# Token lists of a mixture-of-experts layer: scattered into a DRAM table by the router and loaded by GpSimd, in place of lists built on TensorE pass by pass

## The chip, the cores and the metric

One core of one Trainium2 chip. The metric is the device time of one execution of the program in microseconds (us); lower is better.

## The reference

One decoder layer for 512 tokens of 1024 float32 numbers. First comes RMSNorm, an input projection, differential attention and a retention group, and an output projection that is added to x. Then comes the part that the change is about, a mixture of experts:

```
logits = h2 @ w_router + b_router
top_val, top_idx = top_k(logits, 4)          # 4 of 32 experts for each token
gates = softmax(top_val)
# rows of one expert lie together, in blocks of 128 slots
h   = xb @ w_in[e] + b_in[e]                 # 1024 -> 2048
glu = min(h[:, ::2], 7); lin = clip(h[:, 1::2], -7, 7)
act = glu * sigmoid(1.702 * glu) * (lin + 1)
y   = act @ w_out[e] + b_out[e]              # 1024 -> 1024
x   = x + sum over the token's 4 experts of gate * y
```

A last RMSNorm gives the output. There are 512 x 4 = 2048 pairs of token and expert.

## The kernel before

**Stages.** The first 340 us compute attention, retention, the output projection and the router, tile by tile (4 tiles of 128 tokens). The normed rows h2 go to a DRAM table `h2_rows`. Then come the expert passes. A pass is one expert with up to 128 slots, one token in each; with these inputs there are 33 passes (32 experts, one of which needs two). Slots that no token fills are empty. After the last pass the four parts of each token are read back from DRAM, added and normed.

**A pass.** The weights of a pass come as 12 chunks of 1 MB (128 partitions x 2 x 1024 numbers): four for the first half of the up projection, four for the down projection of the pass before, four for the second half. SyncE loads them into a ring of 6 slots, each as soon as the chunk that lay there is used up (`hi_made`, `lo_made`). ScalarE rounds a chunk to float32r (`make_hi`, L1104), VectorE makes the remainder (`make_lo`, L1536), and TensorE multiplies it in 12 matmuls of 512 columns: 8 with the rounded part (L860, L862) and 4 with the remainder (L868). Three buffers of each part let ScalarE run ahead. Every engine walks its passes in a loop of its own (`by_pass`); pass 0 is written out ahead of it, so the loop does passes 1 to 32. The order on each engine is the order of the code; semaphores tie the engines together.

**The list of a pass.** Each pass needs the token, the destination row and the gate of its 128 slots, one slot on each partition. Before the change they are made a pass ahead, in five steps:
1. `prepare_list(p + 1)` on GpSimd (L1729 to L1734) copies the expert's columns out of the router's tables.
2. `slots_one_hot` on VectorE (L1520) compares them with the slot numbers: a 128 x 512 matrix of zeros and ones.
3. `token_list` on TensorE (L827) multiplies it with the four columns of `route`: four matmuls of 4 columns, into the bank that the turned rows use too.
4. `read_list` on VectorE (L1528 to L1531) reads token, destination and gate from there.
5. `gather` on GpSimd (L1748) fetches the 128 rows of h2 by an indirect DMA into `x_rows`. An empty slot fetches row 0.

TensorE turns the rows (`x_transposes`, L835) in the second half of pass p. `keep_lists` on GpSimd (L1761 to L1765) passes the destination and the gate on, through `list_mid`, until ScalarE scales the outputs (`scale_rows`, L1130) and GpSimd scatters them to DRAM (`scatter`, L1755). Destinations of empty slots are out of bounds and are skipped there.

**Router tiles.** In the loop over tiles, VectorE picks the four experts (L1454 to L1459), computes the gates and the columns of `route` (L1461 to L1476); TensorE counts places with triangular matmuls (L778), and VectorE reads them (`read_places`, L1379). After the last tile VectorE makes the table of passes (L1481 to L1512); GpSimd reads it by register loads (`expert_of`).

**Work space.** `work` and `operands` are two views that lie over each other in on-chip memory; x_rows, y_rows and the router's tables are pieces of `work`.

## Time and profile before

| what | value |
|---|---|
| median of 3 executions | 1586.2 us (1584.41 to 1587.89) |
| the profiled execution's own time | 1586.68 us |
| its span in the trace | 1584.9 us |
| TensorE matmul busy | 1506.2 us, 95% of the span |
| VectorE, ScalarE, GpSimd busy | 1321.6, 1008.4, 377.9 us |
| mean granted TensorE clock | 0.967 of full speed |
| passes 1 to 32, time of one | 36.29 us |
| moved by DMA | 476.46 MB |

The span is the time between the first and the last record of the trace; the execution's own time is 1.8 us more. Matmuls are pipelined, so a busy row says that TensorE had work, and the distance between the starts of two matmuls says what one costs.

### The profile page before, as it was taken

To read this page: it belongs to the slowest core of one execution; us is meant where nothing else is said; L and a number is where in the kernel's file an instruction comes from. 1 tells how busy PE (TensorE), PEld (TensorE's weight loads), DVE (VectorE), ACT (ScalarE), POOL (GpSimd) and SP (SyncE) were. 2 spreads that over 40 slices of the span, in tenths; PEclk is the share of its full clock that TensorE was granted. 3 is DMA by queue.
4 is the path that set the end of the run, shared out by engine and by line. 5 is a ranking of instruction groups with operands and counts; after the bars stand their busy time and mean duration, and the time that the engine had idled before them with its cause. 6 is when DMAs were issued, how large, how long until landed. Compare 5 with 4: busy or idle time off the path is not lost.

```text
span 1584.9 us, 23779 instructions
## 1 busy us (share of the span) xinstructions
PE 1506.2 (95%) x7537; PEld 1245.8 (79%) x7537; DVE 1321.6 (83%) x1278; ACT 1008.4 (64%) x898; POOL 377.9 (24%) x382
## 2 busy tenths in 40 slices
PE   7999689979999999999999999999999999999993
PEld 6999368737888888888888888888888888888882
DVE  5641761478999999999999999999999999999998
ACT  5221541236777777777777777777777777777773
POOL 1000301001222233223223222232232232222321
PEclk9999789959999999999999999999999999999997
DMA  9300701018999999999999999999999999999996
GB/s 295 110 1 6 260 1 47 28 42 308 358 365 369 367 369 368 369 375 368 376 360 363 368 366 368 381 358 370 370 380 367 358 365 363 367 373 373 363 375 258
DMA packets 139365, 476.46 MB, mean 301 GB/s; under 512 B 10604, under 2 KB 27272, under 8 KB 139272
## 3 DMA queue, kind: packets, MB, share of 16 engines
q1 hardware_dynamic: 128096, 445.17, 74.7%
q0 software_dynamic: 10496, 28.74, 5.3%
q10 hardware_dynamic: 744, 2.17, 0.3%
q8 instruction: 18, 0.29, 0.1%
q14 instruction: 11, 0.09, 0.0%
HBM read 463.45 MB, written 21.50 MB: 306 GB/s over the span
## 4 chain that ended last, share of the span: by engine, by line
PE 90%; DVE 4%; DMA 3%; issue 2%; ACT 2%; POOL 0%; SPq 0%; DVEq 0%; POOLq 0%; ACTq 0%
PE pair L860 23%; PE pair L868 23%; PE pair L862 23%; PE pair L748 4%; PE pair L604 3%; PE pair L605 3%; PE pair L609 3%; PE pair L875 2%; PE pair L835 2%; PE pair L886 2%; PE pair L827 1%; DMA ring<-in_w_in 1%; PE pair L797 1%; DMA gain_row<-in_ret_norm_g 1%; DVE row_max L1281 1%
## 5 line engine op out<-in xcount | busy, mean ns | idle before, releaser
L1536 DVE TENSOR_TENSOR split<-ring,split 128x2048 fp32r<-128x2048 f32 x396 | 895.0, 2287 | 44.9 <-ACT split L1104 44.8
L1104 ACT CAST split<-ring 128x2048 fp32r<-128x2048 f32 x396 | 757.8, 1914 | 228.4 <-PE pair L868 221.1
L860 PE MATMUL pair<-split,operands 128*128 128x512 f32 x1584 | 633.6, 400 | 2.6 <-DVE operands L1557 1.7
L862 PE MATMUL pair<-split,operands 128*128 128x512 f32 x1584 | 621.1, 392 | 0.0
L868 PE MATMUL pair<-split,operands 128*128 128x512 f32 x1584 | 431.9, 395 | 0.0
L868 PEld LDWEIGHTS pair<-split,operands 128*128 128x128 f32 x1584 | 295.6, 188 | 72.9 <-DVE split L1536 9.2
L860 PEld LDWEIGHTS pair<-split,operands 128*128 128x128 f32 x1584 | 298.5, 188 | 63.9 <-issue 2.2
L862 PEld LDWEIGHTS pair<-split,operands 128*128 128x128 f32 x1584 | 298.5, 188 | 61.0
L1755 POOL DMA_INDIRECT expert_rows<-work,dest_cur x33 | 77.8, 2357 | 372.9 <-PE pair L868 358.3
L1748 POOL DMA_INDIRECT work<-h_rows,token_next x34 | 76.5, 2249 | 301.8 <-DVE token_next L1531 301.8
L604 PE MATMUL pair<-split,operands 128*128 128x256 f32 x352 | 86.1, 282 | 3.1 <-DVE work L1267 3.1
L605 PE MATMUL pair<-split,operands 128*128 128x256 f32 x352 | 85.9, 282 | 0.0
L1110 ACT CAST operands<-pair 128x512 fp32r<-128x512 f32 x66 | 38.7, 587 | 73.3 <-PE pair L868 40.9
L1729 POOL COPY first_cur<-work 128x1 f32 (+1 forms) x34 | 65.6, 1930 | 42.9 <-issue 34.4
L1741 POOL CAST operands<-work 64x128 fp32r x34 | 73.9, 2172 | 1.0 <-PE pair L868 1.0
L604 PEld LDWEIGHTS pair<-split,operands 128*128 128x128 f32 x352 | 67.0, 190 | 3.3 <-DVE work L1267 3.3
L1267 DVE TENSOR_SCALAR work<-pair,stat 128x256 f32<-128x256 f32 x24 | 11.6, 483 | 67.3 <-PE pair L609 67.2
L605 PEld LDWEIGHTS pair<-split,operands 128*128 128x128 f32 x352 | 67.0, 190 | 0.0
L748 PE MATMUL pair<-late_ring,work 128*128 128x256 f32 x256 | 60.5, 400 | 1.7 <-issue 0.8
L998 ACT ACTIVATE work<-pair,stat 128x256 f32<-128x256 f32 x24 | 11.4, 473 | 79.6 <-PE pair L609 75.2
L1761 POOL CAST dest_cur<-list_mid 128x1 int32<-128x1 f32 x33 | 23.3, 706 | 154.3 <-DMA expert_rows<-work,dest_cur 154.3
L748 PEld LDWEIGHTS pair<-late_ring,work 128*128 128x128 f32 x256 | 51.6, 203 | 9.9 <-issue 1.2
(229 smaller groups left out, 1340.9 us busy)
## 6 DMA issues: line engine op xcount, KB each, us to landing
ring<-in_w_moe_in SPq DMA_DIRECT2D x264, 1024.0 KB, 7.9
ring<-in_w_moe_out SPq DMA_DIRECT2D x132, 1024.0 KB, 8.8
ring<-in_w_in SPq DMA_DIRECT2D x12, 1024.0 KB, 9.6
ring<-expert_rows SPq DMA_DIRECT2D x3, 2048.0 KB, 9.1
late_ring<-in_w_o SPq DMA_DIRECT2D x4, 1024.0 KB, 9.6
resid<-in_x SPq DMA_DIRECT2D x4, 512.0 KB, 5.3
h_rows<-work ACTq DMA_DIRECT2D x4, 512.0 KB, 2.6
late_ring<-expert_rows SPq DMA_DIRECT2D x4, 512.0 KB, 5.4
```

The costliest lines, as they stand in the source:

```text
L604: pe.matmul(dst, hT_hi[:, k, at_i], w_hi[s][:, k, :], start=(k == 0), stop=False)
L605: pe.matmul(dst, hT_lo[:, k, at_i], w_hi[s][:, k, :], start=False, stop=False)
L748: mm = pe.matmul(dst, mixT[:, i % 2, k, :], slot(s)[:, k, :], start=(k == 0), stop=(k == KT - 1))
L860: pe.matmul(dst[:, f, :], left_hi[:, k0 + k, :], hi[c.buffer][:, k, cols], start=(start and k == 0), stop=False)
L862: pe.matmul(dst[:, f, :], left_lo[:, k0 + k, :], hi[c.buffer][:, k, cols], start=False, stop=False)
L868: mm = pe.matmul(dst[:, f, :], left_hi[:, k0 + k, :], lo[c.buffer][:, k, cols], start=False, stop=(stop and k == 1))
L1104: act.copy(hi[c.buffer], raw[c.slot]).then_inc(hi_made, 1)
L1536: dve.tensor_tensor(lo[c.buffer], raw[c.slot], hi[c.buffer].bitcast(F32), ALU.subtract).then_inc(lo_made, 1)
L1729: chain(pool.tensor_copy(first_cur[:, :], col(pass_first, p)))
L1741: pool.tensor_copy(pick_bias[0:2 * NE, :], col(expert_rows, e).to_broadcast([2 * NE, SLOTS]))\
L1748: pool.indirect_dma_start(out=x_rows, out_offset=None, in_=h2_dram, in_offset=bass.IndirectOffsetOnAxis(ap=token_next[:, 0:1], axis=0))\
L1755: pool.indirect_dma_start(out=y_dram, in_=y_rows, in_offset=None, out_offset=bass.IndirectOffsetOnAxis(ap=dest_cur[:, 0:1], axis=0), bound ...
```

## The change

**Router.** For each token and each of its four picks, VectorE now computes one entry's address in a DRAM table `slot_lists` (32 experts x 512 rows of 4 words: token, destination, gate, unused): `of_rank`, a 128 x 4 x 32 comparison, replaces the columns of `route`; `place_entries` multiplies it with places and gates (two operations of 128 x 128), sums over experts, and copies the sums out. GpSimd clears the table at the start and scatters the entries by 16 indirect DMAs (four a tile) of 128 entries of 16 bytes. The table of passes gets a second row, `pass_list`, the first row of the list of a pass.

**Passes.** `prepare_list`, `slots_one_hot`, `token_list`, `read_list` and `keep_lists` are gone. GpSimd loads the token column two passes ahead (`load_tokens`: 128 pieces of 4 bytes, 16 bytes apart) and destination and gate for the pass (`load_list`: 128 pieces of 8 bytes); the gather runs two passes ahead of its pass, after TensorE has turned the rows of the pass before. It has a bound now, so empty slots fetch nothing; `x_rows` is cleared once.

**Place.** `work` and `operands` begin directly behind `resid` instead of behind some small tensors.

The diff, cut to its core:

```diff
+        lists_dram = nc.dram_tensor("slot_lists", [LIST_ROWS, 4], I32, kind="Internal").ap()
...
         resid = sb("resid", [P, NT, D])
+        with nc.sbuf_tensor("operands", [P, 20480], F32R) as operands:
+            pass
+        work = sb("work", [P, 21504])
...
-            def token_list(p):
-                pe.wait_ge(onehot_ready, p + 1)
-                for i in range(NT):
-                    mm = pe.matmul(bank[6][:, 0:4], onehot[:, i, :], route_cur[:, i, :],
-                                   start=(i == 0), stop=(i == NT - 1))
-                mm.then_inc(list_ready, 1)
...
                     act_transposes(p - 1, 1)
-                token_list(p + 1)
                 up(p, 0, 3)
...
                 up(p, 1, 1)
-                pe.wait_ge(idx_ready, p + 2)
                 x_transposes(p + 1, 0)
...
-                act.wait_ge(lists_kept, p + 1)
+                act.wait_ge(list_loaded, p * 16)
...
+            def place_entries(i):
+                for a, of_expert_at in enumerate((slot_of, gates)):
+                    chain(dve.tensor_tensor(chosen[:, a], of_rank, of_expert_at[:, i, :].unsqueeze(1).to_broadcast([P, TOPK, NE]),
+                                            ALU.mult))
+                chain.settle()
+                chain(dve.tensor_reduce(chosen_sum, chosen, AX_X, ALU.add))
+                chain.settle()
+                dve.tensor_copy(entry_at[:, i, :], chosen_sum[:, 0, :]).then_inc(entries_ready, 1)
+                dve.tensor_copy(entries[:, i, :, 2].bitcast(F32), chosen_sum[:, 1, :]).then_inc(entries_ready, 1)
...
                 if i:
                     read_places(i - 1)
+                    place_entries(i - 1)
...
                 make_lo(p, 2)
-                slots_one_hot(p + 1)
                 swiglu(p - 1, 1)
                 make_lo(p, 3)
                 make_lo(p, 4)
-                read_list(p + 1)
...
+            def place_entries(i):
+                pool.wait_ge(entries_ready, 2 * (i + 1))
+                for r in range(TOPK):
+                    pool.indirect_dma_start(out=lists_dram, in_=entries[:, i, r, :], in_offset=None,
+                                            out_offset=bass.IndirectOffsetOnAxis(ap=entry_at[:, i, r:r + 1], axis=0))\
+                        .then_inc(entries_placed, 16)
...
+            def load_tokens(p, n):
+                if n is None:
+                    pool.wait_ge(gathered, 16 * p)
+                    pool.sem_inc(pool_passed, 1)
+                c = n or 0
+                pool.dma_start(token_next[:, c:c + 1], list_of(p)[:, 0:1]).then_inc(tokens_loaded, 16)
+
+            def load_list(p):
+                if not (isinstance(p, int) and p == 0):
+                    pool.wait_ge(scattered, p * 16)
+                    pool.sem_inc(pool_passed, 1)
+                pool.dma_start(list_cur[:, :], list_of(p)[:, 1:3]).then_inc(list_loaded, 16)
+
+            def gather(p, n=0):
+                pool.wait_ge(tokens_loaded, 16 * (p + 1))
                 wait(pool, x_transposed, 2 * p)
                 pool.sem_inc(pool_passed, 1)
                 pool.indirect_dma_start(out=x_rows, out_offset=None, in_=h2_dram,
-                                        in_offset=bass.IndirectOffsetOnAxis(ap=token_next[:, 0:1], axis=0))\
-                    .then_inc(gathered, 16)
+                                        in_offset=bass.IndirectOffsetOnAxis(ap=token_next[:, n:n + 1], axis=0),
+                                        bounds_check=SEQ - 1, oob_is_err=False).then_inc(gathered, 16)
...
             def one_pass(p):
                 following = expert_of(p + 1)
-                prepare_list(p + 1, following)
-                gather(p + 1)
                 scatter(p - 1)
                 pick(p + 1, following)
-                pool.wait_ge(scattered, p * 16)
-                pool.sem_inc(pool_passed, 1)
-                keep_lists(True)
+                load_list(p)
+                load_tokens(p + 2, None)
+                gather(p + 2)
```

Before pass 0 GpSimd now does: `place_entries(3)`, the wait for all 16 scatters, `load_tokens(0)`, `gather(0)`, `load_tokens(1)`, `pick(0)`, `load_list(0)`, `gather(1)`, `load_tokens(2)`, `pick(1)`, `gather(2)`.

**Order on TensorE**, first half of a pass of the loop (L860/L862 now L848/L850, L868 now L856, L886 now L874). Before:

```order
L868 MATMUL pair<-split,operands 128x512 x4
L884 ISA
L886 MATMUL pair<-cst,work 128x128 x4
L825 REGISTER_ALU
L827 MATMUL pair<-operands 128x4 x4
L860 MATMUL pair<-split,operands 128x512
```

Now:

```order
L856 MATMUL pair<-split,operands 128x512 x4
L872 ISA
L874 MATMUL pair<-cst,work 128x128 x4
L848 MATMUL pair<-split,operands 128x512
L850 MATMUL pair<-split,operands 128x512
```

The four matmuls of the token list are gone; the turned activations are followed by the next chunk.

**Order on GpSimd**, one pass of the loop (value loads, register steps and branches stand as rows of their own). Before, from the copies of `prepare_list` to `keep_lists`:

```order
L1731 COPY pos_cur<-work 128x4
L128 ISA
L1734 TENSOR_SCALAR slot_from<-pos_cur,first_cur 128x4
L1745 REGISTER_ALU
L128 REGISTER_ALU
L1748 DMA work<-h_rows,token_next 128x1024
L1755 DMA expert_rows<-work,dest_cur 2048x1024
L1739 ISA
L1741 ISA
L1741 COPY operands<-work 64x128
L1773 REGISTER_ALU
L1761 CAST dest_cur<-list_mid 128x1
```

Now, from the scatter to the load of the tokens and the gather:

```order
L1749 DMA expert_rows<-work,list_cur 2048x1024
L1719 ISA
L1721 ISA
L1721 COPY operands<-work 64x128
...
L1736 DMA list_cur<-slot_lists 128x2
...
L1714 TENSOR_LOAD pass_list
L1714 ISA x2
L1730 ISA
L1730 DMA token_next<-slot_lists 128x1
L1739 ISA
L128 REGISTER_ALU
L1742 DMA work<-h_rows,token_next 128x1024
```

The gather stood ahead of the scatter and now stands behind it, at the end of the pass, behind two small loads.

**Order on VectorE**, end of the last router tile. Before:

```order
L1467 RECIPROCAL work<-work 128x1
L1469 TENSOR_SCALAR work<-work 128x32
L1470 TENSOR_SCALAR work<-work 128x32
L1472 TENSOR_SCALAR work<-work 128x32
L1474 CAST work<-work 128x32
L1476 TENSOR_TENSOR work<-work 128x32
L1379 SCALAR_TENSOR_TENSOR work<-pair,work 128x32
L1382 TENSOR_SCALAR work<-work 128x32
L1481 COPY work<-pair 128x32
```

Now:

```order
L1467 RECIPROCAL work<-work 128x1
L1468 TENSOR_TENSOR work<-work 128x128
L1471 TENSOR_SCALAR work<-work 128x32
L1366 SCALAR_TENSOR_TENSOR work<-pair,work 128x32
L1369 TENSOR_TENSOR work<-work 128x32
L1375 TENSOR_TENSOR work<-work 128x128 x2
L1378 TENSOR_REDUCE work<-work 128x8
L1380 CAST work<-work 128x4
L1381 COPY work<-work 128x4
L1477 COPY work<-pair 128x32
```

Four operations of 32 columns give way to one of 128; five operations of `place_entries` now stand between the places and the table of passes.

## Rows read from the trace of the kernel before

**Rows 1.** Stretch, then PE, PEld, DVE, ACT, POOL busy us, clock, DMA share, GB/s.
```profile
600.00:1000.00 400.00, 400.00 (x1853) 327.59 (x1852) 374.32 (x287) 296.56 (x210) 115.43 (x110) 1.00 0.97 368
805.00:810.00 5.00, 5.00 (x23) 3.88 (x22) 5.00 (x3) 4.01 (x3) 0.00 (x0) 1.00 1.02 417
...
340.00:350.00 10.00, 8.51 (x13) 3.24 (x12) 7.39 (x15) 5.50 (x3) 2.96 (x11) 0.50 0.11 25
```

**Rows 2.** Who waited for whom, 600 to 1400: total us, times, longest us.
```profile
ACT split L1104 <- PE pair L868: 145.8, 199, 1.3
...
DVE operands L1520 <- POOL slot_from L1734: 18.5, 22, 0.8
...
PEld pair L868 <- DVE split L1536: 6.5, 22, 0.3
```

**Rows 3.** Chain that ended last, in pass 1: start us, us, what.
```profile
393.16 0.44 PE pair L886 x4
393.60 0.34 PE pair L827 x4
393.94 0.34 PE pair L860
...
411.45 0.24 PE pair L860
```

**Rows 4.** The same chain in pass 32: two lo groups.
```profile
1529.62 0.92 PE pair L868 x4
...
1532.37 1.06 PE pair L868 x4
```

**Rows 5.** GpSimd's timeline, one pass: start us, us, instruction [idle before <-releaser].
```profile
811.12 2.39 POOL L1755 DMA_INDIRECT expert_rows<-work,dest_cur  x1 [11.17 <-PE pair L868]
...
821.01 0.19 POOL L1761 CAST dest_cur<-list_mid 128x1 int32<-128x1 f32 x1 [5.18 <-DMA expert_rows<-work,dest_cur]
...
822.73 2.13 POOL L1729 COPY first_cur<-work 128x1 f32 x1 [1.05 <-issue]
...
833.95 2.28 POOL L1748 DMA_INDIRECT work<-h_rows,token_next  x1 [8.32 <-DVE token_next L1531]
847.41 2.40 POOL L1755 DMA_INDIRECT expert_rows<-work,dest_cur  x1 [11.18 <-PE pair L868]
```

**Rows 6.** DMA issues of the page, median us to landing.
```profile
h_rows<-work ACTq DMA_DIRECT2D x4, 512.0 KB, 2.6
```

**Rows 7.** The gathers' landing time, over all 34.
```profile
DMA to landing us min/median/max: 4.4/10.0/10.7
```

**Rows 8.** TensorE's timeline in the same pass as rows 5: the row turns.
```profile
849.80 0.60 PE L835 MATMUL pair<-cst,work 128*128 128x128 f32 x4
```

**Rows 9.** DMA packets by queue, 800 to 1200.
```profile
q0 software_dynamic: 3168, 8.73, 6.1%
```

**Rows 10.** VectorE's timeline ahead of the expert loop.
```profile
315.53 0.69 DVE L1430 COPY work<-pair 128x512 f32<-128x512 f32 x1 [1.10 <-PE pair L762]
...
334.93 0.23 DVE L1469 TENSOR_SCALAR work<-work 128x32 f32<-128x32 f32 x1
...
336.11 0.19 DVE L1379 SCALAR_TENSOR_TENSOR work<-pair,work 128x32 f32<-128x32 f32 x1
...
340.25 0.19 DVE L1512 TENSOR_SCALAR pass_expert<-pair 1x50 int32<-1x50 f32 x1
```

**Rows 11.** GpSimd's timeline there.
```profile
341.33 0.18 POOL L1729 COPY first_cur<-work 128x1 f32<-128x1 f32 x1 [8.51 <-DVE pass_expert L1512]
...
347.24 1.07 POOL L1748 DMA_INDIRECT work<-h_rows,token_next  x1 [4.31 <-DVE token_next L1531]
```

**Rows 12.** TensorE's timeline in pass 0.
```profile
355.38 0.80 PE L860 MATMUL pair<-split,operands 128*128 128x512 f32 x1 [0.82 <-DVE operands L1541]
...
373.46 0.66 PE L886 MATMUL pair<-cst,work 128*128 128x128 f32 x4 [0.81 <-DVE work L1552]
```

**Rows 13.** Chain that ended last, in pass 0.
```profile
367.83 9.89 DMA work<-h_rows,token_next
```

More of the change, by code:

```diff
@@ L164, in build @@
         last_pass = sb("last_pass", [1, 1], I32)
-        pos_cur = sb("pos_cur", [P, NT])
-        slot_from = sb("slot_from", [P, NT])
-        first_cur = sb("first_cur", [P, 1])
-        token_next = sb("token_next", [P, 1], I32)
-        list_next = sb("list_next", [P, 2])
-        list_mid = sb("list_mid", [P, 2])
-        dest_cur = sb("dest_cur", [P, 1], I32)
-        gate_cur = sb("gate_cur", [P, 1])
-        work_margin = sb("work_margin", [P, 8])
-        with nc.sbuf_tensor("work", [P, 21504], F32) as work:
-            pass
-        operands = sb("operands", [P, 20480], F32R)
+        pass_list = sb("pass_list", [1, IN_TABLE], I32)
+        token_next = sb("token_next", [P, 2], I32)
+        list_cur = sb("list_cur", [P, 2], I32)
+        dest_cur, gate_cur = list_cur[:, 0:1], list_cur[:, 1:2].bitcast(F32)
         def slot(n):
@@ L844, in _ @@
             bias_product(2)
-            token_list(0)
             bias_product(3)
@@ L1781, in _ @@
-            pool.wait_ge(b_in_rounded, 1)
-            pick(0, first)
-            gather(0)
-            pool.sem_inc(gather_started, 1)
-            load_pass_count(pool)
-            keep_lists(False)
-            following = expert_of(1)
-            prepare_list(1, following)
-            gather(1)
-            pool.wait_ge(lists_kept, 1)
-            keep_lists(True)
-            pick(1, following)
-            start = chain.n
-            chain.n = 0
-            def counted_pass(p):
-                chain.before = start + (p - 1) * STEPS_TO_ROUTE
-                one_pass(p)
-                assert chain.n == STEPS_TO_ROUTE, chain.n
@@ L1801, in _ @@
-            by_pass(pool, counted_pass)
-            scatter(after_last(pool) - 1)
-            pool.sem_inc(rows_sent, 1)
+                load_list(p)
+                load_tokens(p + 2, None)
+                gather(p + 2)
+            with nc.allow_non_contiguous_dma(reason="a few hundred words"):
+                place_entries(NT - 1)
+                pool.wait_ge(table_ready, 2)
+                pool.wait_ge(entries_placed, 16 * NT * TOPK)
+                load_tokens(0, 0)
+                first = expert_of(0)
+                gather(0)
+                load_tokens(1, 1)
+                pool.sem_inc(gather_started, 1)
+                pool.wait_ge(experts_listed, 2)
+                pool.wait_ge(b_in_rounded, 1)
+                pick(0, first)
+                load_pass_count(pool)
+                load_list(0)
+                gather(1, 1)
+                load_tokens(2, None)
+                following = expert_of(1)
+                pick(1, following)
+                gather(2)
+                by_pass(pool, one_pass)
+                done = after_last(pool)
+                scatter(done - 1)
+                pool.sem_inc(rows_sent, 1)
+                pool.wait_ge(gathered, 16 * (done + 2))
```

141 lines of the change are left out of this document (58 added, 83 removed).

## The prediction

> **What bounds the kernel now.** I read the busy times by stretch first. From 600 to 1000 TensorE is busy without a gap at full clock, VectorE for 374 of 400 us, and the DMA engines show a share of 0.97 at 368 GB/s [rows 1]. Three resources look full, so the busy shares can't decide. The waits inside the loop can: ScalarE waits for TensorE before 199 chunks, 145.8 us in 800, and for no DMA at all [rows 2]. A weight that came late would show there as a wait of ScalarE's cast for SyncE's queue. So weights are early, and what TensorE executes sets the length of a pass. TensorE itself waits in one place only: once a pass (22 times in 22 passes) a weight load of the remainder group waits up to 0.3 us for VectorE [rows 2]. I then read the chain that ended last, to price single steps on TensorE, and GpSimd's timeline of one pass, whose two scatters give the pass: 847.41 - 811.12 = 36.29 us [rows 5].
>
> **The change part by part.** The sum is made against the profiled execution's own 1586.7 us, which is 0.5 us over the median of 1586.2.
>
> *Token list off TensorE, passes 1 to 32.* In the chain the four matmuls take 0.34 us, and the product behind them starts with 0.34 us where behind the plain turns it starts with 0.24 [rows 3]. So a list costs 0.34 + 0.10 = 0.44 us, and 32 of them 14.1 us. As TensorE is the bound and ran without a gap, this comes off in full, as long as nothing else becomes late.
>
> *The stall on VectorE.* The remainder groups take 0.92 us in the chain, and once a pass one takes 1.06 [rows 4]. That is 0.14 us, 4.5 us over 32 passes. VectorE is behind there since it runs back to back from the list's one-hot on. The change takes the one-hot (0.6 us) and the three small reads (0.35 us) from it, and the 0.8 us in which it waits for GpSimd's copies [rows 2]: it comes to the first remainder after the activation some 1.7 us earlier, and 0.3 us is what it lacks. I take the 4.5 us as gained. Bounds: nothing, if the backlog builds up elsewhere; 0.30 x 32 = 9.6 us, if the whole wait shown is lost time.
>
> *Two small loads a pass, and the gather behind them.* GpSimd scatters at 811.12, copies the bias column, and finds the scatter landed at 821.0 [rows 5]. Then it loads the list and the tokens. A register load and the start of the next instruction take about 1.1 us, and an instruction of GpSimd in the loop some 2.1 to 2.4 us [rows 5]. So the token load is issued by about 821 + 2 x 3.3 = 827.6. The trace shows no such small load; its landing lies between the 2.6 us of a store in a quiet stretch [rows 6] and the 10.7 us of the slowest gather under load [rows 7]. Taking a gather's 10.0, as the load shares its queue and the same busy engines: 837.6, gather issued 837.8, landed 847.8. TensorE turns the rows at 849.80 [rows 8]; the new order leaves that place in the pass as it is. So even the slow end holds by 2 us, and the quick end by 9. Cost: nothing. What hides it is the pass itself; without that cover every microsecond late is one a pass. Queued behind the gather on GpSimd is the next scatter, at 847.41, by when GpSimd has issued the gather 7 us ago. The list for ScalarE is wanted a pass later.
>
> *The gather skips empty slots, and runs a pass earlier.* Of 34 x 128 = 4352 rows some 2050 to 2200 remain, about 9 MB of 476. In the loop the gather is issued at 833.95, lands 10.0 us later and is wanted at 849.80 [rows 5, 7, 8]: it was hidden by 6 us. Nothing is gained but DMA load. A pass would ask for 13.36 - 0.27 = 13.09 MB in 35.71 us, 367 GB/s, where it now moves 368 [rows 1]: the shorter pass and the skipped rows cancel.
>
> *Pass 0.* The second gather is issued at 367.83, late, since its list waits for TensorE; its 9.89 us lie on the chain [rows 13], and TensorE, through with its chunk at 376.65 (373.46 [rows 12], 0.44 for the turns [rows 3] and 2.75 for a chunk, the distance of the two groups [rows 4]), stands for 1.2 us. Now it is issued by about 357: gain 1.2 us. Ahead of that TensorE waits 0.81 us for VectorE's activation [rows 12]; VectorE gets there 0.85 us sooner without its wait for the list. Together 2.0 us.
>
> *Ahead of the passes.* The clock is at 0.50 of full speed here, the 1.2 GHz level, and the DMA share 0.11 [rows 1]. VectorE first. Its operations take 0.19 us for 32 columns and 0.69 for 512 [rows 10], so about 0.29 for 128 and 0.42 for 256; `place_entries` is then 0.2 + 0.29 + 0.42 + 0.1 + 0.17 and three hand-overs of 0.04, 1.3 us. In tiles 1 and 2 it falls into a gap of 1.1 us [rows 10] and shows with 0.2 each; in tile 3 it shows in full, less 0.24, for the dropped columns (334.93 to 336.11 [rows 10]) make room only until TensorE's places are there. With 0.25 us for `pass_list` the table of passes comes 1.7 us later than 340.44 [rows 10]. TensorE's bias products start there, and without the token list between them (0.94 us) end 0.7 us later. By this path the first product starts at 356.1 instead of 355.38 [rows 12]. Now the rows: VectorE gives the last entries free at about 337.9, GpSimd issues four scatters of 1.07 us [rows 11], 342.2, the last lands 3.3 us later (the quickest gather's 4.4 less its issue [rows 7, 11]), 345.5. A register load, 0.9 us (340.44 to 341.33 [rows 10, 11]), then the load of the tokens, 2.6 to 4.4 us [rows 6, 7], then the gather, 4.5: landed at 353.5 to 355.3, first product 2.4 us after that, 355.9 to 357.7. So the cost is 0.7 to 2.3 us; I take 1.5. If GpSimd needs its loaded 2.3 us for each scatter instead of 1.07, add 4.9. The clearing of the table and the longer start on GpSimd (some 1.6 us) lie beside TensorE's output product.
>
> The trace's quickest landings of 2.6 and 4.4 us [rows 6, 7] are the prices I used. The Trainium skill, "DMA: Bandwidth & Descriptors", section "Anatomy of one DMA — SWDGE (gpsimd) path", gives a DMA from GpSimd about 2.0 us plus bytes / 436e3; worked out from it, as an estimate, scatter and load would land in 2.0 us each, and the start would cost 0.7 us instead of 1.5.
>
> *Place of the work space, one-hot, copies.* No row shows an effect of an address on a duration, so I take 0 for the place, with nothing on either side. GpSimd's copies, VectorE's and the waits on them were hidden, but for what is counted.
>
> **The sum.** 1586.7 - 14.1 - 4.5 - 2.0 + 1.5 = 1567.6, some 1567 against the median.
>
> **The rivals.**
> *R1, the stall stays.* VectorE is limited by ScalarE's casts, which follow TensorE, and could end up as late. Then 1586.7 - 14.1 - 2.0 + 1.5 = 1572. For it: 0.14 us is little and the engines are tied; against it: the 1.7 us that it gains.
> *R2, a slow start.* Scatters at 2.3 us each, or slow landings: 5 to 6 us more, 1573, and 1577 if R1 holds too.
> *R3, DMA becomes the bound, slower.* The loads add 256 small packets a pass and 32 for the semaphores. Packets of GpSimd's queue take 6.1% of 16 x 400 us over 3168 packets, 0.123 us each [rows 9]. If a 4-byte packet takes as much as that, 288 x 0.123 / 16 = 2.2 us of all engines a pass come in, and 66 x 0.123 / 16 = 0.5 go out. With a share of 0.97 now [rows 1], 36.29 x 0.97 + 1.7 = 36.9 us would be the pass: +0.6 x 32 = 19 us, 1586.7 + 19 - 0.5 = 1605. It decides where a small packet takes over 0.06 us. Against it: a third of that queue's packets are already small and fill, the share is counted with waiting packets, and there are stretches of 417 GB/s [rows 1].
> The rows can't price a 4-byte packet. The Trainium skill, same page, section "Specifications", wants at least 512 B, below which an engine reads, modifies and writes, and its section "Rules for kernel authors" warns that a strided last dimension becomes one descriptor for each element, as both new loads have it; that speaks for R3.
> *R4, the tokens come late, slower.* If load and gather take over 22 us from 827.6 on, TensorE waits each pass. At 3 us late: 32 x (3 - 0.6) = +77, 1663. Only a landing over 12 us does it; the slowest gather of 34 took 10.7 [rows 7].
> *R5, nothing comes of it.* TensorE's time is filled by another wait (VectorE is busy for 0.94 of the loop): 1585.
>
> **How the numbers follow.** A measurement of this kernel can tell 0.2%, 3.2 us. Chances: forecast 0.58, R1 0.17, R2 0.09, R3 0.08, R4 0.04, R5 0.04. Faster: 0.58 + 0.17 + 0.09 and 0.02 of R5, 0.86; same 0.02; slower 0.12. The range runs from 1561 (the whole 0.3 us stall gained, start at its cheap end: 1586.7 - 14.1 - 9.6 - 2.0 + 0.7 = 1561.7) to 1577 (R1 and R2 together), and leaves out R3 to R5.
>
> **What would show it.** Right: scatters 35.7 us apart in GpSimd's timeline; no remainder group over 0.92 us and no wait of the weight load for VectorE; ScalarE's casts still waiting for TensorE alone; no gap of TensorE near 377; the first product of pass 0 at 356 to 358. Wrong: a wait of the casts for SyncE's queue (R3), of L835's successor for the gather in the loop (R4), four scatters of 2.3 us before pass 0 (R2), a pass of 35.85 (R1). The forecast falls if a pass stays at 36.2 or more.

## The result, and the profile after

| | before | after |
|---|---|---|
| median of the executions | 1587.05 us (1584.41 to 1589.94, 4) | 1565.45 us (1562.15 to 1567.91, 4) |
| ratio to before, 95% interval | | 0.9854, 0.9837 to 0.9870 |
| the profiled execution's own time | 1586.68 us | 1565.79 us |
| its span | 1584.9 us | 1563.9 us |
| a pass, from scatter to scatter | 36.30 us | 35.48 us |
| first product of pass 0 starts | 355.38 us | 363.81 us |
| GpSimd busy | 377.9 us | 220.3 us |
| moved by DMA | 476.46 MB | 467.61 MB |

The change is 1.5% faster. The forecast was 1567 (1561 to 1577), faster. The pass is the mean over 12 scatters from 800 on: (1232.60 - 806.83) / 12 = 35.48. So 32 x 0.82 = 26 us come off in the loop. In these two profiles the first product comes 8.4 us later, of which pass 0 returns 2.9; how much of the 8.4 is the change's is worked out below.

The windows of the changed kernel answer to rows 1 (PE, PEld, DVE, ACT, POOL, clock, DMA share, GB/s):

```profile
60.00:150.00 90.00, 90.00 (x752) 90.00 (x751) 35.77 (x43) 18.78 (x22) 0.00 (x0) 1.00 0.08 24
600.00:1000.00 400.00, 400.00 (x1849) 330.86 (x1848) 372.17 (x250) 303.48 (x215) 52.91 (x57) 1.00 1.00 370
```

The second row looks like the one of before: TensorE full, VectorE 372 of 400, DMA now at 1.00. The first row is one that the prediction never looked at. In the input projection TensorE got through 752 matmuls in 90 us, where the kernel before got through 767:

```profile
60.00:150.00 90.00, 90.00 (x767) 90.00 (x766) 34.50 (x41) 19.04 (x22) 0.00 (x0) 1.00 0.08 24
```

No line of that stage was edited. Only its operands lie elsewhere, and the granted clock was 1.00 in both stretches.

The waits in the loop of the changed kernel, 600 to 1400, in the columns of rows 2:

```profile
ACT split L1091 <- PE pair L856: 130.2, 204, 0.9
POOL work L1742 <- DMA token_next<-slot_lists: 124.8, 22, 6.0
DVE split L1518 <- ACT split L1091: 50.4, 68, 1.1
```

These are three of its lines. The casts of the weights wait for TensorE as before, and for no DMA. The waits of the weight load and of VectorE for GpSimd are gone. GpSimd's timeline of one pass, against rows 5:

```profile
806.83 1.35 POOL L1749 DMA_INDIRECT expert_rows<-work,list_cur  x1 [16.64 <-PE pair L856]
808.15 0.34 POOL L1721 CAST operands<-work 64x128 fp32r x1
816.74 0.58 POOL L1736 DMA_DIRECT2D list_cur<-slot_lists  x1 [8.26 <-issue]
818.12 0.56 POOL L1730 DMA_DIRECT2D token_next<-slot_lists  x1 [0.79 <-issue]
824.42 1.24 POOL L1742 DMA_INDIRECT work<-h_rows,token_next  x1 [5.75 <-DMA token_next<-slot_lists]
842.32 1.34 POOL L1749 DMA_INDIRECT expert_rows<-work,list_cur  x1 [16.65 <-PE pair L856]
```

The token load is issued 11.3 us after the scatter, not 16.5 as I had it, because an instruction of GpSimd takes 0.34 to 1.35 us here and not 2.1 to 2.4. The gather lands some 8 us later (median 8.1 in this stretch), 10 us before the next scatter.

Ahead of pass 0 time was lost. The chain that ended last there (start us, us, what; short links left out at the dots):

```profile
343.46 0.51 DVE work L1375 x2
343.99 0.43 DVE work L1378
...
344.70 0.27 issue
344.96 1.00 POOL slot_lists L1695
345.96 0.30 issue
...
348.80 3.62 DMA slot_lists<-work
352.51 0.51 POOLq L1714
...
353.46 0.55 issue
354.03 1.87 DMA token_next<-slot_lists
...
356.03 0.54 issue
...
356.79 4.29 DMA work<-h_rows,token_next
...
361.22 1.94 PE pair L824 x8
363.16 0.85 PE pair L863 x2
```

It is the path of the prediction: four scatters, the last landing, the register, the token load, the gather, the turns. The scatters stand 1.27 us apart and not 1.07 (0.96 for one, 0.30 between two), and 0.55 us pass ahead of the token load and of the gather each.

### The profile page after: what moved, and what is told of

Its sections match the earlier page's. It is cut to its first block, busy times and chain, and to the rows that moved or that the text cites. A ratio compares the mean times of both kernels' runs of the same rounds, so it can differ in the third digit from the quotient of the medians.

```text
span 1563.9 us, 23287 instructions
## 1 busy us (share of the span) xinstructions
PE 1483.7 (95%) x7401; PEld 1237.8 (79%) x7401; DVE 1294.1 (83%) x1151; ACT 1009.3 (65%) x898; POOL 220.3 (14%) x237
## 2 busy tenths in 40 slices
DMA packets 142278, 467.61 MB, mean 299 GB/s; under 512 B 15702, under 2 KB 32370, under 8 KB 142185
## 4 chain that ended last, share of the span: by engine, by line
PE 90%; DVE 3%; DMA 3%; ACT 2%; issue 2%; POOL 0%; SPq 0%; POOLq 0%; DVEq 0%; ACTq 0%
PE pair L848 23%; PE pair L850 23%; PE pair L856 23%; PE pair L745 4%; PE pair L601 3%; PE pair L602 3%; PE pair L606 3%; PE pair L824 2%; PE pair L863 2%; PE pair L874 2%; DMA ring<-in_w_in 1%; DMA gain_row<-in_ret_norm_g 1%; DVE row_max L1268 1%; PE pair L767 0%; PE pair L794 0%
## 5 line engine op out<-in xcount | busy, mean ns | idle before, releaser
L848 PE MATMUL pair<-split,operands 128*128 128x512 f32 x1584 | 631.0, 398 | 1.7 <-DVE operands L1539 1.7
L850 PE MATMUL pair<-split,operands 128*128 128x512 f32 x1584 | 618.9, 391 | 0.0
L856 PE MATMUL pair<-split,operands 128*128 128x512 f32 x1584 | 424.4, 390 | 0.0
L856 PEld LDWEIGHTS pair<-split,operands 128*128 128x128 f32 x1584 | 297.5, 188 | 63.2
L848 PEld LDWEIGHTS pair<-split,operands 128*128 128x128 f32 x1584 | 298.2, 188 | 61.3 <-issue 2.2
L850 PEld LDWEIGHTS pair<-split,operands 128*128 128x128 f32 x1584 | 298.4, 188 | 58.6
L1749 POOL DMA_INDIRECT expert_rows<-work,list_cur x33 | 44.7, 1353 | 513.9 <-PE pair L856 507.9
L601 PE MATMUL pair<-split,operands 128*128 128x256 f32 x352 | 88.1, 287 | 3.4 <-DVE work L1254 3.4
L602 PE MATMUL pair<-split,operands 128*128 128x256 f32 x352 | 87.8, 286 | 0.0
L1097 ACT CAST operands<-pair 128x512 fp32r<-128x512 f32 x66 | 38.8, 588 | 74.4 <-PE pair L856 41.4
L1736 POOL DMA_DIRECT2D list_cur<-slot_lists x33 | 19.1, 580 | 267.9 <-issue 267.9
L1111 ACT CAST operands<-pair 128x512 fp32r<-128x512 f32 x66 | 38.6, 584 | 24.5 <-PE pair L874 24.5
L1534 DVE SCALAR_TENSOR_TENSOR work<-work 128x512 f32<-128x512 f32 x66 | 45.7, 692 | 6.9
```

The lines of the kernel that those rows point to most:

```text
L601: pe.matmul(dst, hT_hi[:, k, at_i], w_hi[s][:, k, :], start=(k == 0), stop=False)
L602: pe.matmul(dst, hT_lo[:, k, at_i], w_hi[s][:, k, :], start=False, stop=False)
L848: pe.matmul(dst[:, f, :], left_hi[:, k0 + k, :], hi[c.buffer][:, k, cols], start=(start and k == 0), stop=False)
L850: pe.matmul(dst[:, f, :], left_lo[:, k0 + k, :], hi[c.buffer][:, k, cols], start=False, stop=False)
L856: mm = pe.matmul(dst[:, f, :], left_hi[:, k0 + k, :], lo[c.buffer][:, k, cols], start=False, stop=(stop and k == 1))
L1534: dve.scalar_tensor_tensor(result, gate, ACT_LIMIT, line, ALU.min, ALU.mult).then_inc(act_ready, 1)
```

## The experiments

Each kernel is the changed one with the edit shown, but for the first, which is the kernel before. A difference of two kernels is taken from their ratios to the kernel before, or from the pass where the loop alone is meant; a pass repeats within 0.02 us from profile to profile where nothing touched it.

### The place alone

```diff
 resid = sb("resid", [P, NT, D])
+with nc.sbuf_tensor("operands", [P, 20480], F32R) as operands:
+    pass
+work = sb("work", [P, 21504])
...
-with nc.sbuf_tensor("work", [P, 21504], F32) as work:
-    pass
-operands = sb("operands", [P, 20480], F32R)
```

> The kernel before with nothing but the new place of work and operands. Theory P (the place sets TensorE's pace): the input projection takes 283 ns a matmul instead of 279 and GpSimd's row loads of norm2 start 3.8 us later, as in the changed kernel, and a chunk of 12 matmuls takes 2.72 us instead of 2.75; scatters 36.0 us apart, total 1587 + 3.8 - 10 = about 1581. Theory L (the lighter loop makes the matmuls quicker and the early 3.8 us are scatter between programs): both stay as before, 1587.

Measured: 1592.23 us, ratio 1.0020 (1.0003 to 1.0036); 752 matmuls in the projection, as in the changed kernel. So the projection's slower pace is the place's; as the pass is unchanged, the whole loss, 0.20% or 3.2 us (0.5 to 5.7), lies ahead of the loop. The chunks of the loop went from 2.75 to 2.72 us, but the pass stayed at 36.31: the stall grew. Waits, 600 to 1400:

```profile
PEld pair L867 <- DVE split L1535: 11.0, 22, 0.5
PEld pair L885 <- DVE work L1551: 2.3, 15, 0.2
```

6.5 us before, 13.3 now. A quicker TensorE would catch up with VectorE sooner; that fits, but no run varied it by itself.

### The change at the old place

```diff
-with nc.sbuf_tensor("operands", [P, 20480], F32R) as operands:
-    pass
-work = sb("work", [P, 21504])
...
+with nc.sbuf_tensor("work", [P, 21504], F32) as work:
+    pass
+operands = sb("operands", [P, 20480], F32R)
```

> The changed kernel with work and operands back at their old address. Theory P: the projection gains its 3.8 us back (279 ns), the loop goes to 2.75 us a chunk and 35.75 us a pass: 1565.5 - 3.8 + 8.5 = about 1570. Theory L: 1565.5, a pass stays at 35.49 us.

Measured: 1568.74 us, ratio 0.9880 (0.9863 to 0.9897), 767 matmuls, chunks of 2.75 us, no wait of a weight load. The pass is 35.69 us, what the prediction's terms give (35.71), and the first product comes at 358.66. So the place gives 0.21 us a pass once the stall is gone. Against the changed kernel the ratio is 0.0026 higher, 4.1 us, where the loop alone gives 6.7; so the place takes some 2.6 us ahead of the passes, in line with the run above. The two first products lie 5.1 us apart, but that is one profile against another, with different granted clocks (see the account of the prediction).

### The four matmuls back

```diff
                 if before:
                     act_transposes(p - 1, 1)
+                    for i in range(NT):
+                        pe.matmul(bank[6][:, 0:4], xT_hi[:, i, :], xT_lo[:, i, 0:4], start=(i == 0), stop=(i == NT - 1))
                 up(p, 0, 3)
```

> The changed kernel with four matmuls of 4 columns at the place of the token list in passes 1 to 32, with nothing to wait for (their product is not used). If the list's cost was TensorE's time alone, 0.44 us a pass: 1565.5 + 14.1 = 1579.6 and scatters 35.93 us apart. If its cost was what hung on it (the waits of other engines), under 5 us more.

Measured: 1579.28 us, ratio 0.9931 (0.9916 to 0.9946), a pass of 35.90 us. The list's matmuls cost 0.42 us, 13.4 us in all, though nobody waits for them. The timeline shows it (products between them left out): from the turns to the next remainder group 2.72 us, where the changed kernel takes 2.28.

```profile
829.88 0.60 PE L874 MATMUL pair<-cst,work 128*128 128x128 f32 x4
830.24 0.59 PE L890 MATMUL pair<-operands 128*128 128x4 f32 x4
...
832.60 1.07 PE L856 MATMUL pair<-split,operands 128*128 128x512 f32 x4
```

### VectorE's work back, without its wait

```diff
                 make_lo(p, 2)
+                chain(dve.tensor_tensor(spare, pass_number.to_broadcast([P, 512]), pass_number.to_broadcast([P, 512]), ALU.is_equal))
                 swiglu(p - 1, 1)
                 make_lo(p, 3)
                 make_lo(p, 4)
+                for n in range(3):
+                    chain(dve.tensor_scalar(spare[:, n:n + 1], pass_number, 1.0, None, ALU.add))
```

> The changed kernel with one operation of 128 x 512 at the place of the one-hot and three of one column at the place of the list's reads on VectorE, without any wait on GpSimd (their results are not used). If VectorE's backlog made the stall, part of it comes back: weight loads wait for VectorE's remainder once a pass, a remainder group takes over 0.92 us, and the total is 2 to 4.5 us over 1565.5. If the 0.8 us in which it waited for GpSimd was what made it late, nothing comes back: 1565.5.

Measured: 1564.49 us, ratio 0.9846 (0.9829 to 0.9862), a pass of 35.48. VectorE is busy 380 of 400 us, and TensorE waits for it nowhere. By itself the work that the change takes off VectorE was worth nothing.

### And its wait for GpSimd

```diff
+                dve.wait_ge(copied, 4 * p)
...
+            def make_copies():
+                for n in range(4):
+                    pool.tensor_copy(copies[:, n:n + 1], pass_number).then_inc(copied, 1)
...
                 load_tokens(p + 2, None)
+                pool.wait_ge(copied, 4 * p)
+                pool.sem_inc(pool_passed, 1)
+                make_copies()
                 gather(p + 2)
```

The first line stands ahead of the 128 x 512 operation of the run above.

> The changed kernel with VectorE's one-hot and three small operations back, as in the run before, and now also four small copies on GpSimd ahead of the gather, for which the one-hot waits. Theory, the stall of the kernel before was made by VectorE's wait for GpSimd and not by its extra work (which alone cost nothing, 1564.5): the wait of 0.1 to 0.8 us once a pass returns, with it a wait of a weight load for VectorE of up to 0.3 us, and a remainder group of 1.03 to 1.06 us: +0.14 x 32 = 4.5 us, 1570. Rival, the stall needed the token list's coupling of TensorE to VectorE (bank read, list): no remainder group over 0.92, 1565.

Measured: 1576.38 us, ratio 0.9933 (0.9908 to 0.9957), a pass of 35.79, +0.31. Waits, 600 to 1400:

```profile
DVE work L1552 <- POOL copies L1762: 12.6, 23, 2.3
PEld pair L859 <- DVE split L1521: 8.7, 22, 0.8
```

Once a pass the weight load waits again, and the timeline has a group of 1.04 us (838.41 to 839.45, where others take 0.91; rows between left out):

```profile
835.60 1.07 PE L859 MATMUL pair<-split,operands 128*128 128x512 f32 x4
...
838.41 1.20 PE L859 MATMUL pair<-split,operands 128*128 128x512 f32 x4
839.45 0.62 PE L866 MATMUL pair<-operands 128*128 128x512 f32 x2
```

VectorE does the same work as in the run above. New are the wait, 0.55 us on the mean, and the four small copies on GpSimd that it waits for. So this wait, on top of that work, makes such a stall, and the rival (that the list's bank is needed for it) falls. A run with the wait and without the work was not made. The price is near twice what I expected. One long wait is not the reason: of twelve passes one takes 36.39 us, the other eleven 35.74 on the mean, 0.26 more than without the wait, while VectorE waits 0.43 to 0.46 us in nine of the ten passes from 786 to 1108. The reason is nearer the place: the 0.14 us were read at the old place, and at the new one the kernel before stalls more (the run with the place alone: 36.31 - 35.48 - 0.42 = 0.41 us a pass).

### All rows gathered

```diff
+            pool.memset(no_entries.rearrange("p (n c) -> p n c", c=4)[:, :, 0].bitcast(F32), 0.0).then_inc(tokens_named, 1)
```

> The changed kernel with the empty slots' token set to 0, so that every gather moves all 128 rows again (34 x 128 = 4352 rows in place of some 2100, +9 MB). Theory, the skip is worth nothing because the gather is hidden and weights are early: 1565.5 within 3 us, no wait of ScalarE's casts for a DMA, gathers in the loop landing at 8 to 10 us in place of 8.1. Rival, the skip is what keeps the shorter pass within the DMA engines' reach (share 1.00 at 370 GB/s in the loop): casts wait for SyncE's queue and the pass grows from 35.49 towards 35.49 x 377/370 = 36.2 us, 1587.

Measured: 1564.98 us, ratio 0.9855 (0.9829 to 0.9881), a pass of 35.48, 377 GB/s at a share of 1.00, no wait of a cast for a DMA. The skip of empty slots is worth nothing, and a share of 1.00 at 370 GB/s isn't the limit of the DMA engines.

### Four more small loads a pass

```diff
                 pool.dma_start(token_next[:, c:c + 1], list_of(p)[:, 0:1]).then_inc(tokens_loaded, 16)
+                if n is None:
+                    for m in range(4):
+                        pool.dma_start(more[:, m:m + 1], lists_dram[0:SLOTS, m % 3:m % 3 + 1]).then_inc(more_loaded, 16)
```

> The changed kernel with four more loads of 128 x 4 bytes a pass on GpSimd's queue (512 more small packets beside 256). It prices a small packet. Theory, small packets fit between the large ones and weights have room: 1565.5 within 3 us, pass 35.49 us, no DMA wait; the token load and the gather land later by a few us, still hidden. Rival, by the price of my prediction, 0.123 us a packet on 16 engines: 512 x 0.123 / 16 = 3.9 us of all engines a pass; with the share at 1.00 now, all of it would be lost, 32 x 3.9 = +126 us, 1691; half that price still gives 1628.

Measured: 1560.72 us, ratio 0.9827 (0.9802 to 0.9852), its interval overlaps that of the changed kernel; a pass of 35.48 again. The packets of GpSimd's queue, 800 to 1200, first the changed kernel, then this one:

```profile
q0 software_dynamic: 3872, 5.80, 4.1%
```

```profile
q0 software_dynamic: 5424, 5.99, 4.4%
```

These 400 us cut passes differently in the two profiles (5.80 and 5.99 MB). Over twelve whole passes of each, 806.83 to 1232.60 and 800.43 to 1226.20, the queue has 4224 and 5760 packets at 4.1% and 4.3%: 48 loads bring 1536 packets, 32 for a load and not 128, though it has 128 pieces of 4 bytes. They take 0.2% of 16 x 426 us, some 0.009 us a packet (0.004 to 0.013, as the shares are rounded), a tenth or less of the price that the rival used and about a seventh of the 0.06 at which it decides. The small pieces that the Trainium skill warns of ("DMA: Bandwidth & Descriptors", "Rules for kernel authors") are harmless at this number: by the rows, five such loads a pass cost no time.

### 64 and 128 bytes further

```diff
 resid = sb("resid", [P, NT, D])
+place_margin = sb("place_margin", [P, 16])
 with nc.sbuf_tensor("operands", [P, 20480], F32R) as operands:
```

> The changed kernel with work and operands 64 bytes further (131264 in place of 131200); the old place was 142400. It tells what in the place sets TensorE's pace. Theory A, the position within 128 bytes: the old place and this one are both 64 past a multiple of 128, so the input projection goes back to 279 ns a matmul and 767 matmuls in 60 to 150, the loop to chunks of 2.75 us, total near that of the run at the old place, 1568.7. Theory B, something coarser (the distance from the split parts, or the region): 283 ns, 752 matmuls and 2.72 us stay, 1565.5.

> The changed kernel with work and operands 128 bytes further (131328), the one remainder of 256 not yet seen (0). Seen so far, address by remainder: 64 gives 767 matmuls and 2.75 us a chunk, 128 gives 752 and 2.72, 192 gives 797 and 2.80. If projection and chunk always trade places, 0 gives either more than 797 with over 2.80 (slower, over 1586) or under 752 with under 2.72; if the pattern is one of 128 bytes with a coarser part on top, about 752 to 760 and 2.72 to 2.74, 1565 to 1572. No theory here says which; the run fills the table.

Measured: 1585.91 us, ratio 0.9979 (0.9963 to 0.9996), and 1585.89, ratio 0.9987 (0.9975 to 1.0000). An empty margin of 64 bytes eats nearly the whole change. Windows of the 64-byte run:

```profile
60.00:150.00 90.00, 90.00 (x797) 90.00 (x796) 36.09 (x44) 19.07 (x22) 0.00 (x0) 1.00 0.08 24
600.00:1000.00 400.00, 400.00 (x1809) 323.59 (x1808) 366.40 (x243) 296.32 (x210) 54.21 (x55) 1.00 0.99 362
```

And two remainder groups of neighbouring chunks in its loop, 2.80 us apart, where the changed kernel's are 2.72 apart:

```profile
827.78 1.09 PE L857 MATMUL pair<-split,operands 128*128 128x512 f32 x4
...
830.58 1.09 PE L857 MATMUL pair<-split,operands 128*128 128x512 f32 x4
```

The projection is quicker than anywhere (797), the pass slower (36.30 us; 36.19 in the 128-byte run, whose projection has 761). The output projection doesn't take part: its matmuls take 395 ns in place of 409, but the run with all rows gathered and the one with four more loads, both at the changed kernel's place, have 395 too. In them the granted clock from 270 to 320 was 1.00, where the changed kernel's profile has 0.86. Position within 128 bytes (theory A of the first text) is refuted: the old place shares it with the 64-byte run and has neither its 797 nor its 2.80 us. So is a coarse cause.

### The projection's weights alone moved

Here and below, the weights of a matmul are the 128 x 128 operand that a weight load puts into TensorE. In the input projection these are the turned input rows (hT), in the expert passes the turned rows and activations (xT, actT); the numbers of the layer's own weight matrices stream past them.

```diff
-hT_hi, hT_lo = (operands[:, a:a + KT * SEQ].rearrange("p (k t) -> p k t", k=KT) for a in (12288, 16384))
+hT_hi, hT_lo = (operands[:, a:a + KT * SEQ].rearrange("p (k t) -> p k t", k=KT) for a in (12240, 16336))
```

> The changed kernel with only the turned rows of the input projection (hT_hi, hT_lo, the matmuls' weights there) 192 bytes earlier, so that they lie 192 past a multiple of 256 bytes as in the run with the 64-byte shift; the expert passes' operands stay. Theory, the pace of a stage follows where its own matmul weights begin, in steps of 64 bytes: the projection goes to 797 matmuls in 60 to 150 (752 now), later stages start 5 to 6.5 us earlier (norm2's load at about 258.5 in place of 264.63), chunks stay at 2.72 us: 1565.5 - 6 = 1559.5. Rival, something else in the moved region sets it (results, tables, other tensors): 752 matmuls, 1565.

Measured: 1558.06 us, ratio 0.9793 (0.9779 to 0.9807), below the interval of the changed kernel. The projection has 796 matmuls in its 90 us, the pass stays at 35.48, GpSimd's load of the gains of the second RMSNorm (L1661), the first mark behind attention, starts at 259.14 in place of 264.63, the first product at 359.04 in place of 363.81.

```profile
60.00:150.00 90.00, 90.00 (x796) 90.00 (x795) 36.39 (x45) 19.48 (x23) 0.00 (x0) 1.00 0.08 24
```

### The expert operands moved back inside the 64-byte shift

```diff
 def halves(a):
-    return operands[:, a:a + KT * SLOTS].rearrange("p (k t) -> p k t", k=KT)
+    return operands[:, 48 + a:48 + a + KT * SLOTS].rearrange("p (k t) -> p k t", k=KT)
...
-b_in_parts = operands[:, 4096:4096 + 2 * FF]
+b_in_parts = operands[:, 4144:4144 + 2 * FF]
...
-pick_bias = operands[:, 6144:6144 + SLOTS]
+pick_bias = operands[:, 6192:6192 + SLOTS]
```

> The run with the 64-byte shift once more, but the expert passes' own operands (the turned rows and activations, xT and actT, and the bias parts and pick) another 192 bytes further inside it, so that they start 256 bytes behind where the changed kernel has them, while everything else keeps the 64-byte shift. It tells whose place sets the chunk's pace. Theory, the place of the matmul's weights: chunks back at 2.72 us, the pass 35.5 us, the projection still at 797 matmuls in 60 to 150; the 64-byte shift then keeps its earlier start alone: 1585.9 - 32 x 0.82 = 1560, at best 1556. Rival, another tensor in the moved region (bank results' readers, the activations' rows, the tables behind): chunks stay at 2.80 us, the pass at 36.3 us, 1586.

Measured: 1554.57 us, ratio 0.9810 (0.9768 to 0.9852), a pass of 35.47, chunks of 2.72, the projection still at 797. Together with the run before: of the moved region, the place of the matmuls' own weights sets the pace, stage by stage. The bias parts and the pick moved with them here, but no matmul of a chunk reads those. All that was seen, by where the stage's weights start (remainder of the address by 256 bytes):

| remainder | matmuls of the projection, 60 to 150 | a chunk of the loop, us |
|---|---|---|
| 0 (128-byte run) | 761 | 2.80 |
| 64 (old place) | 767 | 2.75 |
| 128 (changed kernel) | 752 | 2.72 |
| 192 (64-byte run) | 797 | 2.80 |
| the projection's alone at 192 | 796 | 2.72 |
| the operands' alone at 128 | 797 | 2.72 |

The remainder is a label and not a mechanism: what is best for the projection (192) is worst for the loop. Why is open; which bytes other engines touch at that time was not varied. Remainder 64 was seen only at the old place, 11 KB further on.

### A version that beats both

The changed kernel with hT as above, the turned rows of the output projection and the router 64 bytes further, and the first list's register load ahead of the wait for the scatters:

```diff
-mixT = w(12288, 2 * D).rearrange("p (b k t) -> p b k t", b=2, k=KT)
-b_in_rows = w(14336, 2 * FF, 2 * NE)
-w_router_sb = w(16384, KT * NE).rearrange("p (k e) -> p k e", k=KT)
+mixT = w(12304, 2 * D).rearrange("p (b k t) -> p b k t", b=2, k=KT)
+b_in_rows = w(14352, 2 * FF, 2 * NE)
+w_router_sb = w(16400, KT * NE).rearrange("p (k e) -> p k e", k=KT)
...
+                early = list_of(0)
                 pool.wait_ge(entries_placed, 16 * NT * TOPK)
-                load_tokens(0, 0)
+                pool.dma_start(token_next[:, 0:1], early[:, 0:1]).then_inc(tokens_loaded, 16)
```

> A version meant to beat both: the changed kernel with the projection's weights moved as in the run e10, the turned rows of the output projection and the router (mixT) moved by 64 bytes likewise (with two loaded tables behind it), and the register load of the first list's row ahead of the wait for the scatters. From the runs so far: -6 us for the projection, some -2 for the output projection (its matmuls took 395 ns in place of 409 at that place), -0.5 to -0.9 for the register load ahead of pass 0, which would show in the trace as a token load issued 0.5 us after the last scatter landed in place of 1.5: 1557, within 4 for the time at which the clock rises. If the moved weights of the projection are without effect: 1564.

Measured: 1555.03 us, ratio 0.9797 (0.9784 to 0.9811). Its chain ahead of pass 0:

```profile
337.74 3.99 DMA slot_lists<-work
...
341.88 0.55 issue
342.45 2.05 DMA token_next<-slot_lists
```

From the last scatter's landing to the token load 0.72 us pass (341.73 to 342.45), where the changed kernel took 1.61 (352.42 to 354.03): 0.9 us less in this step. Over the whole way, from VectorE's last reciprocal in the router to the first product, it doesn't show: 21.63 us here, 21.86 in the changed kernel, 21.27 in the run above, which has no such edit. The output projection's matmuls take 398 ns in place of 409, which the granted clock alone can do (see the 64-byte run). So of the three edits only the projection's place is shown to gain. This version and the two above can't be told apart by their intervals. Each beats the kernel before by about 2%. Their ratios lie 0.4 to 0.6% below the changed kernel's; for this one and the one with the projection's weights moved the intervals lie apart from its own.

## Why the prediction was right

By its own terms, against the pass and the first product of the profiles:

| term | forecast, us | measured, us | from |
|---|---|---|---|
| token list off TensorE | -14.1 | -13.4 | 0.42 x 32, the four matmuls back |
| stall on VectorE | -4.5 | -6.1 | what is left: 36.30 - 35.69 - 0.42 = 0.19, x 32 |
| place, in the loop | 0 | -6.7 | 35.69 - 35.48 = 0.21, x 32 |
| ahead of the router's last tile: place, and scatter of the profiles | 0 | +7.1 | VectorE's last reciprocal, 341.95 - 334.85 |
| router and first gather | +1.5 | +1.3 | from there to the first product, 21.86 - 20.53 |
| pass 0 | -2.0 | -2.9 | bias of pass 1: 384.46 to 390.01, +5.5 of 8.4 |
| sum | -19.1 | -20.7 | 1586.7 - 20.7 = 1566.0; it was 1565.8 |

The rows ahead of the loop rest on one profile of each kernel, and the granted clock differs between profiles. Some of them side by side; the reciprocal (L1467 in both kernels) belongs to the gates of the last tile:

| run | place | clock, 270 to 320 | output projection, ns a matmul | last reciprocal, us | from there to the first product |
|---|---|---|---|---|---|
| before | old | 0.93 | 400 | 334.85 | 20.53 |
| place alone | new | 0.93 | 400 | 341.01 | 20.52 |
| change at the old place | old | 1.00 | 395 | 336.27 | 22.39 |
| changed kernel | new | 0.86 | 409 | 341.95 | 21.86 |
| four matmuls back | new | 0.86 | 406 | 342.55 | 22.06 |
| VectorE's work back | new | 0.86 | 409 | 343.40 | 22.13 |
| all rows gathered | new | 1.00 | 395 | 337.95 | 21.88 |
| four more loads | new | 1.00 | 395 | 336.80 | 22.16 |

At one place and with the same code on TensorE up to there, the reciprocal comes between 336.80 and 343.40. So a difference of two first products is not the place's price.

**The bound.** TensorE set the pass and does so after: every run's pass follows what TensorE executes. A resource that shows 95 to 100% busy beside it (VectorE at 380 of 400, DMA at 1.00) was not a bound, as the runs with added work on each show.

**Token list.** Right to 0.02 us a pass, from the difference of two starts in the chain.

**Stall.** Right in kind and near in size, within its bounds of 0 to 9.6 us, but the step behind it was half wrong. I counted the one-hot, the small reads and the wait together as what VectorE gains. The work alone made no stall; with the wait for GpSimd on top it came back. So VectorE has slack for 0.95 us of work, and not for the wait as well. The size depends on the order in which stall and place are taken: at the new place the stall is 0.41 us a pass, 13.1 us, and the place alone gives nothing in the loop (36.30 to 36.31). Both orders add up to 12.8 us.

**Small loads and the gather.** Hidden, as forecast, with more room than forecast: the token load was issued 5 us sooner and took 5.3 us (median) and not 10. The limit that I set by a gather's landing was safe and far off. R3 falls with the packets' price, R4 with 10 us of room.

**Place of the work space.** This is the step that failed: "No row shows an effect of an address on a duration, so I take 0 for the place, with nothing on either side." No row of one kernel could show it. Its part in the loop is -6.7 us. Its part ahead of the loop is about +3 by the medians (3.2 with the place alone, 2.6 from the change at the old place); the rest of the 7.1 us in the table is scatter of single profiles, to which the granted clock, different from one to the next, is the likely reason and not a shown one. The two parts cancel in part, so the total hid part of the error. That 64 bytes more would have cost 20 us (ratio 0.9979) shows how lucky the zero was; R5's result would have come, by a mechanism that no rival had.

**Start.** Right: +1.3 us in the changed kernel's profile and 1.9 at the old place, inside the bounds of 0.7 to 2.3. Every link of the path is in the chain, and the rows landed 19.1 us after the last reciprocal (361.08) where the forecast's 353.5 to 355.3 mean 18.7 to 20.5. Inside it two errors cancel, which is luck. Too small were the gaps between instructions of GpSimd: 0.30 us between two scatters and 0.55 ahead of a DMA whose address comes from a register or a wait, three to four of them. Too large was the token load: 1.87 us against 2.6 to 4.4; here the Trainium skill's 2.0 us ("DMA: Bandwidth & Descriptors", "Anatomy of one DMA — SWDGE (gpsimd) path") was nearer than my rows, though in the loop, under load, the same load takes 5.3. The other landings were priced well: 3.6 us for the scatter (forecast 3.3), 4.3 for the gather (4.5).

**Pass 0.** TensorE's gap at the second gather (0.98 us) is gone, as forecast. Its wait for the activation, which the forecast took off whole, only shrank, from 0.81 to 0.49 us. Most of the rest of the 2.9 us are the list's matmuls in pass 0 (0.4 us), which the sum left out, and 0.8 us in the first chunk (5.17 us before, 4.41 now), which ran at the 1.2 GHz level for less long.

## What to carry to other kernels

Where one engine is the bound, a few tiny instructions on it cost their full time on every turn of the loop, and work on a neighbour that looks 95% busy may cost nothing; look for the neighbour's waits, not its work. When an edit moves a tensor from which TensorE loads its weights, measure the edit with the tensors held in their places as well, or the place's effect (here -6.7 us in the loop, about +3 ahead of it or, 64 bytes on, +26 us in the loop) is taken for the edit's. Before a difference ahead of the full stretch is put down to an edit, compare the granted clock of the two profiles there. Time in hand from a tuned place is cheap: one offset gave 0.6% more (0.9793 against 0.9854).

## What was not expected of the hardware

**The place of a matmul's weights** changes its pace by up to 6% (752 to 797 matmuls in 90 us) and a chunk's by 3% (2.72 to 2.80 us), in steps of 64 bytes, and not in the same direction for two stages. A third, the output projection, shows none: 395 ns a matmul at each of the remainders 0, 64, 128 and 192, in profiles with a granted clock of 0.96 to 1.00 from 270 to 320. The Trainium skill states ("SBUF — State Buffer", section "SBUF: two separate sides") that of the engines only VectorE and GpSimd contend for a port and TensorE never waits on anyone. The runs don't show what TensorE waits for; they do show that its pace depends on an address, which that rule doesn't foresee.

**GpSimd's instructions** take 1.33 us for the scatter and 0.34 for the pick (the copy of the bias column, L1721) where they took 2.40 and 2.34 in the kernel before. The groups of the changed kernel, 600 to 1400 (busy us, mean ns):

```profile
L1749 POOL DMA_INDIRECT expert_rows<-work,list_cur x22 | 29.2, 1327 | 344.6 <-PE pair L856 344.6
L1721 POOL CAST operands<-work 64x128 fp32r x22 | 7.4, 338 | 0.0
```

With VectorE's old work back the scatter takes 2087 ns again, with its wait back the pick 2293. They are the same instructions: what they meet on VectorE changes, and their time with it.

**The clock's rise** in pass 0 moved. In the profile of the changed kernel TensorE stood idle for 4.5 us before the first turns and ran its first chunk at the 1.2 GHz level until 367.46. In the run that gathers all rows, with the same code on TensorE, the granted clock was 0.97 in 360 to 365 already. Ahead of the passes the granted clock differs between profiles too, 0.86 or 1.00 from 270 to 320. That is part of why executions of one kernel lie 5 us apart and why no term under 3 us can be read from one total or from one first product.
